# Attention in a two-layer hybrid decoder step: transposes over two PSUM banks, score banks by kind of item, decode sums divided after the value product

## The reference, cut to what matters

```python
# windowed (dilated) and differential attention in the mixers, then cross-attention
s = einsum(q, k) * scale + bias          # masked
p = exp(s - max(s)) / sum(exp(s - max(s)))
o = einsum(p, v)                         # differential: p of map 0 minus lambda * p of map 1
```

## Time and profile before

| | us |
|---|---|
| median of 3 runs | 2038.75 (2037.47 to 2040.96) |
| profiled execution | 2039.49, of which span 2037.8 |
| PE busy in the span | 1807.9 (89%) |
| DVE, ACT busy | 950.7 (47%), 668.5 (33%) |
| mixer attention, layers 0 and 1 | about 372 to 487 and 1379 to 1494 |
| cross attention, layers 0 and 1 | about 668 to 725 and 1674 to 1732 |

### The profile page before, as it was taken

How to read it: one execution, slowest core, us unless ns; L and a number is a source line. 1 busy time by engine, 2 the same in 40 slices (tenths; PEclk the granted TensorE clock), 3 DMA queues, 4 the chain that set the end, 5 groups by cost and what they waited for, 6 DMA issues and landing times.

```text
span 2037.8 us, 29711 instructions
## 1 busy us (share of the span) xinstructions
PE 1807.9 (89%) x12182; PEld 1625.1 (80%) x12182; DVE 950.7 (47%) x1519; ACT 668.5 (33%) x915; POOL 114.3 (6%) x220
## 2 busy tenths in 40 slices
PE   7999999778889779999989999896788896799997
PEld 6999987445777568999889999783468774799997
DVE  5454354443554354544455543453445444545434
ACT  3332242332333224332243322432322341333323
POOL 0000100000000000000100001000000000000010
PEclk9999989776898988999989999897768888899998
DMA  7443453665253542443424435436653436234342
GB/s 238 150 144 122 149 207 107 211 261 236 87 172 116 210 162 92 156 138 129 168 83 144 152 121 171 176 124 238 256 199 104 152 138 248 83 124 152 137 133 78
DMA packets 62891, 319.28 MB, mean 157 GB/s; under 512 B 8922, under 2 KB 11354, under 8 KB 37706
## 3 DMA queue, kind: packets, MB, share of 16 engines
q0 software_dynamic: 31104, 205.53, 29.4%
q1 hardware_dynamic: 31690, 112.36, 14.9%
HBM read 307.08 MB, written 10.79 MB: 156 GB/s over the span
## 4 chain that ended last, share of the span: by engine, by line
PE 81%; DVE 9%; ACT 4%; DMA 3%; issue 2%; SPq 0%; ACTq 0%; DVEq 0%; POOLq 0%
PE ps L566 20%; PE ps L567 20%; PE ps L568 20%; PE ps L533 6%; PE ps L835 3%; PE ps L669 2%; PE ps L670 2%; PE ps L671 2%; DMA ring<-in_ckv 2%; PE ps L752 1%; DVE bn L1332 1%; DVE arena L1493 1%; PE ps L862 1%; DVE m_low L1293 1%; DVE w_low L1286 1%
## 5 line engine op out<-in xcount | busy, mean ns | idle before, releaser
L566 PE MATMUL ps<-x_high,w_high 128*128 128x320 f32 x1408 | 440.1, 313 | 14.9 <-DVE w_low L1286 7.9
L567 PE MATMUL ps<-x_low,w_high 128*128 128x320 f32 x1408 | 438.8, 312 | 0.0
L568 PE MATMUL ps<-x_high,w_low 128*128 128x320 f32 x1408 | 438.8, 312 | 0.0
L1019 ACT ACTIVATE w_high<-ring 128x2048 fp32r<-128x2048 f32 (+1 forms) x152 | 256.7, 1691 | 476.9 <-PE ps L568 476.1
L1286 DVE TENSOR_TENSOR w_low<-ring,w_high 128x2048 fp32r<-128x2048 f32 (+1 forms) x152 | 305.5, 2010 | 161.0 <-ACT w_high L1019 160.8
L566 PEld LDWEIGHTS ps<-x_high,w_high 128*128 128x128 f32 x1408 | 268.0, 190 | 16.4 <-issue 14.0
L567 PEld LDWEIGHTS ps<-x_low,w_high 128*128 128x128 f32 x1408 | 268.0, 190 | 0.0
L568 PEld LDWEIGHTS ps<-x_high,w_low 128*128 128x128 f32 x1408 | 267.7, 190 | 0.0
L566 PE MATMUL ps<-h_high,w_high 128*128 128x320 f32 x704 | 219.9, 312 | 6.1 <-DVE h_low L1314 6.1
L1293 DVE TENSOR_TENSOR m_low<-ring,m_high 128x1024 fp32r<-128x1024 f32 x112 | 137.0, 1224 | 187.0 <-ACT m_high L1065 187.0
L505 POOL DMA_DIRECT2D ring<-in_w x216 | 114.1, 529 | 1885.4 <-PE ps L568 1293.6
(11 more groups left out here) (284 smaller groups left out, 2501.4 us busy)
## 6 DMA issues: line engine op xcount, KB each, us to landing
ring<-in_w POOLq DMA_DIRECT2D x152, 1024.0 KB, 5.2
ring<-in_w POOLq DMA_DIRECT2D x64, 704.0 KB, 4.3
cache<-in_dkv SPq DMA_DIRECT2D x64, 256.0 KB, 5.8
ring<-in_dkv SPq DMA_DIRECT2D x64, 256.0 KB, 4.6
cache<-in_ckv SPq DMA_DIRECT2D x8, 2048.0 KB, 9.7
ring<-in_ckv SPq DMA_DIRECT2D x8, 2048.0 KB, 7.6
cache<-in_wkv SPq DMA_DIRECT2D x8, 1536.0 KB, 7.9
ring<-in_wkv SPq DMA_DIRECT2D x8, 1536.0 KB, 7.8
```

Of the source, the lines that this page charges most:

```text
L566: mm(out, wh, xh, start=first, stop=False)
L567: mm(out, wh, xl, start=False, stop=False)
L568: return mm(out, wl, xh, start=False, stop=last)
L1019: fn(w_high[:, pos % 2, 0:n], ring[:, pos % RING, 0:n], ACT.Copy).then_inc(hi_w.sem, 1)
```

## The change

It touches the attention stages only; the order of items on every engine stays.

1. T batches alternate between banks 5 and 6, by a running count. A batch waits for the copy of the batch before the last one, no longer for the last.
2. Scores of decode items go to banks 0 to 2, those of prompt items to banks 3 and 4 (`SCORES_AT`), instead of by even and odd. S waits for the maxima (in the cross stage the exponentials) of the last item of its own kind.
3. For decode items N only forms the reciprocal (and for d the sign), into a new tile `weights`. The pass over the probabilities is gone; T waits for `e_done` instead of `p_done`, and O multiplies mask and weight in one `scalar_tensor_tensor`.
4. V of `cross_dec` alternates between banks 1 and 2.
5. PE's wait for `tm_dve` 9 before the mixer stage moves behind S of items 0 and 1, ahead of T of item 0.
6. On PE the waits of T are plain waits: the separate increment of the counter `passed` behind them (`wait_apart`) is gone.

```diff
+DECODE = [k[-3:] == "dec" for k, _ in ITEMS]
+PROMPTS = [DECODE[:i + 1].count(False) for i in range(NI)]
+SCORES_AT = [0 if d else 3 for d in DECODE]
...
                 def scores(i, first):
-                    b0 = 3 * (i % 2)
-                    if i - 2 >= first:
+                    b0 = SCORES_AT[i]
+                    before = [j for j in range(first, i) if DECODE[j] == DECODE[i]]
+                    if before:
                         s = m_done if kind[:5] != "cross" else e_done
-                        pe.wait_ge(s.sem, s.upto(l, i - 1))
+                        pe.wait_ge(s.sem, s.upto(l, before[-1] + 1))
...
                 def transposes(i, first):
-                    wait_apart(pe, "pe", p_done.sem, p_done.upto(l, i + 1))
+                    if DECODE[i]:
+                        pe.wait_ge(e_done.sem, e_done.upto(l, i + 1))
+                    else:
+                        pe.wait_ge(p_done.sem, p_done.upto(l, PROMPTS[i]))
                     for b in range(BATCHES[i]):
-                        if i > first or b:
-                            wait_apart(pe, "pe", t_done.sem, t_done.upto(l, BEFORE[i] + b))
+                        turn = BEFORE[i] + b
+                        if turn >= BEFORE[first] + 2:
+                            pe.wait_ge(t_done.sem, t_done.upto(l, turn - 1))
+                        bank = 5 + turn % 2
...
-                        bank = 1 + 3 * (i % 2)
+                        bank = 1 + n % 2
...
-                pe.wait_ge(tm_dve.sem, tm_dve.upto(l, 9))
                 pe.wait_ge(q_built.sem, q_built.upto(l, 1))
-                attention(0, len(MIXER))
+
+                def rows_out():
+                    pe.wait_ge(tm_dve.sem, tm_dve.upto(l, 9))
+                attention(0, len(MIXER), rows_out)
...
                 def normalise(i):
+                    if DECODE[i]:
+                        w = weights[:, turn(i):turn(i) + 1]
+                        link(V.reciprocal(w, st[:, 8:9]))
+                        if kind == "diff_dec":
+                            link(V.tensor_tensor(w, w, sign, ALU.mult))
+                        return
...
                     if kind == "diff_dec":
-                        last = V.tensor_tensor(view(own_d[n], [[P, 2], [1, P]]), view(ps[:, 7, 0:1], [[0, 2], [1, P]]),
-                                               view(heads_d, [[P, 2], [1, P]]), ALU.mult)
+                        last = V.scalar_tensor_tensor(view(own_d[n], [[P, 2], [1, P]]), view(ps[:, 7, 0:1], [[0, 2], [1, P]]),
+                                                      weight, view(heads_d, [[P, 2], [1, P]]), ALU.mult, ALU.mult)
```

More of the change, by code:

```diff
@@ L165, in build @@
         stat = sb("stat", [P, 2, 16])
+        weights = sb("weights", [P, 4])
         small = sb("small", [P, 64])
@@ L293, in build @@
         e_done = signal("e_done", NI)
-        p_done = signal("p_done", NI)
+        p_done = signal("p_done", PROMPTS[-1])
         t_psum = signal("t_psum", NB)
@@ L809, in transposes @@
                                 for kb in range(2):
-                                    last = tr(ps[:, 6, 256 * kb + P * qb:256 * kb + P * qb + P],
+                                    last = tr(ps[:, bank, 256 * kb + P * qb:256 * kb + P * qb + P],
                                               p[:, 256 * qb + P * kb:256 * qb + P * kb + P])
@@ L813, in transposes @@
                             for c in range(3):
-                                last = tr(ps[:, 6, P * c:P * c + P], p[:, P * c:P * c + P])
+                                last = tr(ps[:, bank, P * c:P * c + P], p[:, P * c:P * c + P])
                         last.then_inc(t_psum.sem, 1)
@@ L875, in own_heads, with attention @@
                     last.then_inc(o_psum.sem, 1)
-                def attention(first, end):
+                def attention(first, end, before_transposes=None):
                     scores(first, first)
@@ L882, in attention @@
                             scores(i + 1, first)
+                        if i == first and before_transposes:
+                            before_transposes()
                         transposes(i, first)
@@ L1476, in maxima, with turn @@
                         V.tensor_scalar(st[0:r1, 4:4 + k], st[0:r1, 0:k], -XSCALE, None, ALU.mult).then_inc(m_done.sem, 1)
+                def turn(i):
+                    return DECODE[:i].count(True) % 4
                 def normalise(i):
@@ L1502, in outputs @@
                     kind, n = ITEMS[i]
+                    weight = weights[:, turn(i):turn(i) + 1]
                     dve.wait_ge(o_psum.sem, o_psum.upto(l, i + 1))
                     if kind == "diff_dec":
-                        last = V.tensor_tensor(view(own_d[n], [[P, 2], [1, P]]), view(ps[:, 7, 0:1], [[0, 2], [1, P]]),
-                                               view(heads_d, [[P, 2], [1, P]]), ALU.mult)
+                        last = V.scalar_tensor_tensor(view(own_d[n], [[P, 2], [1, P]]), view(ps[:, 7, 0:1], [[0, 2], [1, P]]),
+                                                      weight, view(heads_d, [[P, 2], [1, P]]), ALU.mult, ALU.mult)
                     elif kind == "win_dec":
-                        last = V.tensor_tensor(view(own_w[n], [[P, 2], [1, P]]), view(ps[:, 7, 0:1], [[0, 2], [1, P]]),
-                                               view(heads_w, [[P, 2], [1, P]]), ALU.mult)
+                        last = V.scalar_tensor_tensor(view(own_w[n], [[P, 2], [1, P]]), view(ps[:, 7, 0:1], [[0, 2], [1, P]]),
+                                                      weight, view(heads_w, [[P, 2], [1, P]]), ALU.mult, ALU.mult)
                     elif kind == "win_pro":
@@ L1536, in own_heads @@
                     dve.wait_ge(xv_psum.sem, xv_psum.upto(l, n + 1))
-                    V.tensor_tensor(own_x[i % 2].rearrange("p (h d) -> p h d", h=2),
-                                    ps[:, 1 + 3 * (i % 2), :].rearrange("p (h d) -> p h d", h=2),
-                                    view(heads_x, [[1, 2], [0, 256]]), ALU.mult).then_inc(xv_done.sem, 1)
+                    V.scalar_tensor_tensor(own_x[i % 2].rearrange("p (h d) -> p h d", h=2),
+                                           ps[:, 1 + n % 2, :].rearrange("p (h d) -> p h d", h=2), weights[:, turn(i):turn(i) + 1],
+                                           view(heads_x, [[1, 2], [0, 256]]), ALU.mult, ALU.mult).then_inc(xv_done.sem, 1)
                 def attention(first, end):
```

33 lines of the change are left out of this document (15 added, 18 removed).

## The result

| | before | after |
|---|---|---|
| median of the runs | 2039.51 (2037.47 to 2040.96, 4 runs) | 1977.55 (1969.59 to 1979.80, 4 runs) |
| profiled execution (span) | 2039.49 (2037.8) | 1979.60 (1977.9) |
| mean granted clock | 0.911 | 0.933 |
| PE busy | 1807.9 | 1771.5 |

The ratio is 0.9695, with a 95% interval of 0.9678 to 0.9712: 62 us faster. The row of the page that I should have expected least is the one on PE: the same 12182 instructions are busy 36 us less.

What follows compares the result with a forecast made beforehand. The mixer stage was taken as a loop with one engine working at a time. Gains of 20.3 us in layer 0, 18.2 in layer 1 and 2 for the clock made 40.5: 2038.75 to 1998.2, range 1985 to 2010.

Steps and rivals of the forecast that it cites:

- I put 2 in all: Mixer stage, V of decode items: some V may keep full clock with shorter pauses; 2 us in all, bounds 0 to 6.
- the full clock for most V: Rival: most V of decode items in the mixer stage at full clock, 19.6 us more, 1979; chance 0.22.
- chain terms: Gains from shorter waits along the attention stages, clock apart: 20.3 us in layer 0 and 18.2 in layer 1, cross stages included.
- the head: Start of the mixer stage up to V of d0: earlier scores, no pass, overlapped transposes; 6.4 us in each layer.
- Two banks: T to V of d0: two transpose batches run back to back, 3.1 us instead of 4.49, 1.4 gained.
- d3: Mixer stage, item d3: the dropped pass and the shorter T to V, not behind a load; 2.9 us in each layer.
- The load is late next: Mixer stage: scores of d3 come 14.8 to 15.7 us after V of d1, as before, losing most of d2's gain of 3.0.
- a reserve of 1.7: Mixer stage, x items: loads take some 9 us of the 10.7 left, so they stay hidden by 1.7 us.
- the rival of the pacing loads: Rival: loads set the pace nearly throughout the mixer stage; 2020, or 2010 if half of them do; chance 0.13.
- The cross stage: T of cross items no longer waits 0.49 us for the normalising pass, twice on the path; 0.9 us in each layer.
- The small ones: Prompt T without the counter increment gains 0.5 us a layer; O's new instruction costs 0; cross stage gains 0.9 a layer.
- The slower rival: Rival: the clock falls in the cross stage, a pair of items taking some 6 us more; 2054; chance 0.04.

Runs made afterwards that it cites:

- the two filled kernels: Kernel before and kernel after, each with unread identity products put in PE's pauses, not in the same places: 2007.85 us and 1970.52 us.
- Quarter loads: Kernel after with the loads of d2, d3 and all four x items bringing only a quarter of their columns: 1963.50 us.
- the banks alone: Kernel before with transposes over two banks, score banks by kind and plain waits, normalising pass and early wait kept: 2013.01 us.
- one filling: Kernel after with unread products: 12 ahead of the first T, 20 in the wait for d2, 6 before each x item's scores: 1977.66 us.

## Why the prediction was wrong

**The step that failed is the clock's: "I put 2 in all".** V alone got 21.0 us shorter, the scores 5.6, and the stretches between mixer and cross stage, which I had at nothing, 7.7. Net of the waits that this brought, the clock comes to 24 to 29 us. The rival "the full clock for most V", 1979 at a chance of 0.22, named the mechanism, and the choice against it was wrong. That its number fits to 1.5 us is in part luck. Its bound of 21.6 counts V of three d items of four, and no scores and no retention: V of all decode items at full clock takes 34.6 us for 60.3, 25.7 less. What the bound left out was about made up by waits for loads in the mixer stages, 0.6 us before and 16.0 after. I chose by the earlier trace rows: V at 0.50 and the stage at 0.74. But those rows show the clock *with* the pauses that the change takes out. They are the state to be changed, not evidence that it stays. The rows that bore on the choice were the pauses: 3.63 ahead of T of d0, 1.94 at d1, 0.8 between batches, set against what was left of them (2.42, 0.40 and 0.25 in the trace after). Nor did I ask of the clock what I asked of the loads, who else is served by it: retention follows V(x3) on the same clock.

**The chain** was close in sum. At a held clock the change gives 32.9 us in the mixer stages and 2.8 in the cross stages (traces of the two filled kernels), for chain terms of 36.7 and 1.8. Singly: the head gave 7.4 in layer 0 and 6.9 in layer 1 for 6.4. The scores followed ACT's last copy by 0.1 us and T the exponential's end, as forecast; from T to V it took 2.3 and 2.7 us where I had 3.1. Two banks gave 2.0 to 2.8 from T to V for a d item and 1.8 for an x item (2.4 for one), where I had 2.4 to 3.2 and 1.9 to 2.3; the short times are those at full clock, where T and V of d1 wait 0.25 and 0.36 us for a copy. The dropped pass: T of decode items waits for DVE no more. PE's stretch from the scores of d0 to the end of V(x3) went from 114.6 to 88.4 us in layer 0, below the 95 to 97 that I had named as a sign of being right.

**d3** was put at 2.9 and gave 6.7 in layer 0: scores 1.92 for 3.64 and V 2.3 for 4.2 make 3.6 of the other 3.8. It is the clock again, in the segment where the whole of it showed.

**The loads.** "The load is late next" was right in kind and wrong in place. I had the scores of d3 wait 2 to 3 us in both layers and the load of d2 "just fit", because V(d1) ended 15.0 after V(d0). At full clock it ended 12.7 after it, and the wait fell on d2: 3.8 and 3.5. For the x items I left a reserve of 1.7; the faster V used it up, 4.3 and 4.4 us of waits. So the rival of the pacing loads came true in part as well, as a consequence of the clock. Quarter loads price the greater part of it at 14 us.

**The cross stage** gave 1.7 and -0.2 for 0.9 each: the waits for its loads grew from 4.4 to 7.7 and took the rest.

**The small ones.** `scalar_tensor_tensor` in O was put at nothing by the wrong row. The scalar of L1339 is a constant, the one in O is a column of a tile. With a tile's column it takes 484 ns, where the `tensor_tensor` before took 424, and 751 for 691 in the cross stage: 1.4 us over 24 instructions. How much of it lies on the path is not shown. The trace of before had rows that fit:

```profile
L1603 DVE SCALAR_TENSOR_TENSOR tok<-ps,small,hid 128x128 f32<-128x128 f32 x16 | 4.3, 344 | 0.1
...
L1576 DVE TENSOR_TENSOR arena<-ps,decay 128x128 f32<-128x128 f32 x8 | 2.2, 280 | 0.0
```

Here, too, the column (`small`) costs some 60 ns; with a constant (L1595, the same shape) it was 281.

**The slower rival** and the rule of the Trainium skill behind it ("TensorE: Matmul & The Clock Gate", section "A second HAM failure mode: psum-queue depth-cycling") did not come. The banks alternate now, and the clock is higher: 0.84 for 0.74 over 372 to 487 us, and 0.920 for 0.911 over the span already with the banks alone. The cross stages hold 1.00 in both layers, as before.

## What to carry to other kernels

A stage of short matmuls that ran at the lower clock is a reason to expect more than the sum of the pauses from a change that shortens them: price every matmul of the stage, and of the stage behind it, at full clock too, and choose between the two sums by how long the pauses will be, not by the clock that they give today. Before a forecast, look for what the faster engine asks for next (here the load of the item after next): it will be late sooner than the old spacing says. And a few unread products in a pause that can't be removed are a cheap test of the clock. Whether they are a gain is read from the stage behind as well: here one filling gained 5.1 us in its stages and lost 5.2 behind them.

## What the hardware showed that I had not expected

- Products that nobody reads made the kernel before 31 us (1.5%) faster: V of a d item took 1.96 for 3.64 with the pauses around its transposes filled.
- On the kernel after, fillings that left V(x3) and retention at the lower clock gave nothing in all; with fillings there too it was 7 us.
- The queue of SP needs 8.2 to 10.1 us to issue the 16 transfers of a pair (d2 and d3, all traces), whether each brings 64 or 256 KB. On two queues the issue takes about half of that, each transfer takes longer, and the pair of 4.2 MB lands no sooner.
- A `scalar_tensor_tensor` whose scalar is a tile's column took some 60 ns longer than a `tensor_tensor` of its shape (484 for 424, 751 for 691); with a constant as the scalar it took no longer (281 and 280, 489 and 487).
